# Value products ahead of the next transposes in the attention steps of a two-block transformer kernel

## The reference, cut to what matters

```python
# l0: differential attention, 8 heads, two softmaxes a head
sc = einsum('bqhcd,bkhcd->bhcqk', q_blk, k) * scale
sc = where(causal_mask(i, s), sc + bias, NEG_INF)
a = softmax(sc, axis=-1)
wts = a[:, :, 0] - lam * a[:, :, 1]
return einsum('bhqk,bkhv->bqhv', wts, v)
# l1: latent attention, 16 heads: softmax(where(causal, qn.kn + qp.kp)) @ v
# a:  grouped attention, 16 heads on 4 key heads; 256 tokens see 256 context
#     keys and 256 own keys, and 256 context rows see the 256 context keys
# b:  neighbourhood attention, 16 heads; 256 own keys with a bias, 256 context keys
p = softmax(concatenate([s_nb, s_cx], axis=-1), axis=-1)
return einsum('bqhk,bqkhd->bqhd', p[..., :n_nb], vw) + einsum('bhqs,bshd->bqhd', p[..., n_nb:], vc)
```

## Time and profile before

| | us |
|---|---|
| median of 3 runs | 1422.12 |
| the profiled execution, its own time | 1420.74 |
| its span in the trace | 1418.9 |
| TensorE busy in the span | 1317.7 (93%) |
| VectorE busy | 910.9 (64%) |
| ScalarE busy | 683.4 (48%) |
| granted TensorE clock, mean | 0.981 of full speed |

### The profile page before, as it was taken

The page is one execution under the profiler, slowest core; times in us unless marked ns, Lnnn a source line. Parts: engine busy times, 40 slices in busy tenths (PEclk is TensorE's granted clock), DMA queues, the critical chain, the costliest instruction groups (busy, mean ns, idle before and its releaser), DMA issues.

```text
span 1418.9 us, 24879 instructions
## 1 busy us (share of the span) xinstructions
PE 1317.7 (93%) x9164; PEld 1150.6 (81%) x9164; DVE 910.9 (64%) x1398; ACT 683.4 (48%) x1191; POOL 369.1 (26%) x388
## 2 busy tenths in 40 slices
PE   6989999999998999898999999999989898999777
PEld 4867799999988886798999999788745578889446
DVE  6858667777766887557777778354277437533864
ACT  5554445555544776435555545234376324124651
POOL 5921134333332050232433342111011210000011
PEclk9999999999999999999999999999999998999999
DMA  8565546655643542264656664132200353334100
GB/s 291 177 223 173 181 134 210 183 185 178 182 128 104 164 138 86 102 213 135 218 179 180 186 192 169 60 104 90 89 16 1 83 154 91 103 104 134 30 1 30
DMA packets 52367, 191.58 MB, mean 135 GB/s; under 512 B 6016, under 2 KB 6272, under 8 KB 51904
## 3 DMA queue, kind: packets, MB, share of 16 engines
q1 hardware_dynamic: 43344, 158.85, 36.0%
q0 software_dynamic: 8368, 31.33, 7.1%
q10 hardware_dynamic: 576, 0.31, 0.1%
HBM read 189.41 MB, written 1.05 MB: 134 GB/s over the span
## 4 chain that ended last, share of the span: by engine, by line
PE 76%; DVE 10%; issue 7%; ACT 5%; POOL 1%; DMA 1%; SPq 0%; ACTq 0%; DVEq 0%; POOLq 0%
PE G L394 14%; PE G L396 13%; PE G L395 13%; PE A L394 5%; PE A L396 5%; PE A L395 5%; PE R L514 4%; PE R L559 3%; DVE WL L951 2%; ACT WH L1529 2%; DVE SM L1017 1%; PE A L859 1%; PE R L394 1%; PE G L923 1%; PE R L396 1%
## 5 line engine op out<-in xcount | busy, mean ns | idle before, releaser
L951 DVE TENSOR_TENSOR WL<-RAW,WH 128x1024 fp32r<-128x1024 f32 x295 | 388.2, 1322 | 339.5 <-ACT WH L1529 339.2
L1529 ACT ACTIVATE WH<-RAW 128x1024 fp32r<-128x1024 f32 x295 | 310.4, 1057 | 474.0 <-PE G L396 351.2
L394 PE MATMUL G<-XH,WH 128*128 128x256 f32 (+1 forms) x1408 | 423.7, 301 | 22.6 <-DVE XL L1310 7.5
L395 PE MATMUL G<-XL,WH 128*128 128x256 f32 (+1 forms) x1408 | 420.3, 298 | 0.0
L396 PE MATMUL G<-XH,WL 128*128 128x256 f32 (+1 forms) x1408 | 420.3, 298 | 0.0
L394 PEld LDWEIGHTS G<-XH,WH 128*128 128x128 f32 x1408 | 271.0, 192 | 34.7 <-issue 14.6
L395 PEld LDWEIGHTS G<-XL,WH 128*128 128x128 f32 x1408 | 270.9, 192 | 7.6
L396 PEld LDWEIGHTS G<-XH,WL 128*128 128x128 f32 x1408 | 270.9, 192 | 7.6
L394 PE MATMUL A<-HH,WH 128*128 128x256 f32 x352 | 99.8, 283 | 0.0
L395 PE MATMUL A<-HL,WH 128*128 128x256 f32 x352 | 99.6, 283 | 0.0
L396 PE MATMUL A<-HH,WL 128*128 128x256 f32 x352 | 99.6, 283 | 0.0
(11 more groups left out here) (321 smaller groups left out, 2266.6 us busy)
## 6 DMA issues: line engine op xcount, KB each, us to landing
RAW<-in_wst SPq DMA_DIRECT2D x295, 512.0 KB, 3.7
M<-in_wmod POOLq DMA_DIRECT2D x48, 512.0 KB, 4.6
B<-in_rpb POOLq DMA_DIRECT2D x4, 1024.0 KB, 10.8
H<-in_x_t SPq DMA_DIRECT2D x2, 512.0 KB, 9.2
M<-in_x_tok SPq DMA_DIRECT2D x1, 1024.0 KB, 12.8
M<-in_ctx_t POOLq DMA_DIRECT2D x1, 1024.0 KB, 5.2
out_y<-M SPq DMA_DIRECT2D x1, 1024.0 KB, 3.9
C<-in_cst SPq DMA_DIRECT2D x1, 737.0 KB, 14.7
```

The source lines that it names most:

```text
L394: mm(out, lh, rh, start=start, stop=False, skip_group_check=True)
L395: mm(out, lh, rl, start=False, stop=False, skip_group_check=True)
L951: v.tensor_tensor(WL[:, slot, :], RAW[:, raw, :], WH[:, slot, :].bitcast(F32), ALU.subtract).then_inc(w_lo, 1)
L1529: act(WH[:, slot, :], RAW[:, raw, :], ACT.Copy).then_inc(w_hi, 1)
```

## The change

In `attention` on TensorE the block that issues the value products of unit n-3 is put between the filler and the transposes of unit n-2. Their waits go with them. No other engine's list changes; nothing is added or left out.

```diff
@@ -548,6 +548,13 @@
                         scores(A[2 * (a % 2):2 * (a % 2) + 2], units[n]).then_inc(at_s, 1)
                     if n < len(units) + 2:
                         fill(filler)
+                    if n >= 3 and units[n - 3][4]:
+                        p, qt, nk, job, last = units[n - 3]
+                        pe.wait_ge(at_tc, AU0[s] + n - 2)
+                        j = AJ0[s] + job
+                        if j >= 2:
+                            pe.wait_ge(at_g, j - 1)
+                        value(G[j % 2], att(s, j), units[n - 3]).then_inc(at_pv, 1)
                     if 2 <= n <= len(units) + 1:
                         nk = units[n - 2][2]
                         a = AU0[s] + n - 2
@@ -559,13 +566,6 @@
                                 m = nc.tensor.transpose(ST[c][:, k * P:(k + 1) * P],
                                                         PRB[a % 3][:, c, k * P:(k + 1) * P], IDT)
                         m.then_inc(at_t, 1)
-                    if n >= 3 and units[n - 3][4]:
-                        p, qt, nk, job, last = units[n - 3]
-                        pe.wait_ge(at_tc, AU0[s] + n - 2)
-                        j = AJ0[s] + job
-                        if j >= 2:
-                            pe.wait_ge(at_g, j - 1)
-                        value(G[j % 2], att(s, j), units[n - 3]).then_inc(at_pv, 1)
```

## The result

| | kernel before | changed kernel |
|---|---|---|
| median, first comparison | 1422.12 us (5 runs) | 1428.08 us (5 runs, 1424.98 to 1429.40) |
| ratio, 95% interval | | 1.0051 (1.0034 to 1.0067) |
| median, second comparison | 1421.77 us (21 runs) | 1426.30 us (10 runs, 1422.36 to 1429.16) |
| ratio, 95% interval | | 1.0032 (1.0017 to 1.0047) |
| span of the profiled execution | 1418.9 us | 1426.3 us |

The forecast was 1426.3 us, a loss of 4.2. The medians differ by 6.0 us in the first comparison and by 4.5 in the second. Both intervals lie above 1, so the changed kernel is slower, if only by 0.3 to 0.5%. That the second median is the forecast to the digit is luck: the two medians of the changed kernel lie 1.8 us apart.

What follows compares the result with a forecast made beforehand. Each stage was taken as bound by its closed chain of releases, with TensorE busy for most of the span. Stage a +7.14, its end +0.7, stage b -3.6, l0 and l1 0: +4.2 on 1422.12 gives 1426.3 us, range 1422 to 1431.

Steps and rivals of the forecast that it cites:

- Which chain closes in stage a: Stage a: ten steps through copies, exponentials, transposes and the 16 records make the 10.45 us period; the 8 records are outside.
- The 8 records: Stage a: put ahead, they delay the next u0's transposes by 1.02 us a period, to 11.47; 7 x 1.02 = 7.14.
- The 16 records cost nothing: Stage a: u2's value products and u3's short transposes wait for the same copy, so swapping them costs 0.
- The slack for the delayed exponentials of u1: Stage a: exponentials come 1.45 us later but end 0.7 before VectorE asks; without that slack, up to 10 us in 7 periods.
- The end of a: End of stage a: TensorE waits for the last short copy between the two last value groups, +0.7 us.
- Stage b: Value products fill TensorE's wait; period 7.08 to 6.50 us, then closed over ScalarE; five times plus 0.7 at the end, -3.6.
- b gives nothing: Rival, stage b: later copy and exponentials on ScalarE keep the loop as long as before; 1429.9 us, chance 0.14.
- l0 and l1: Stages l0 and l1: 0 each, as l1's chain holds nothing that moves and l0's TensorE is nearly always busy.
- The copies in a are not what holds it: Rival, stage a: the 8 records cost nothing and b's gain stands; 1418.5 us, chance 0.09.
- waits filled everywhere: Rival, stages a and b: value products fill TensorE's idle time and no other chain closes; -11.4, 1410.7 us, chance 0.03.
- The sum: Whole kernel: 7.14 + 0.7 - 3.6 = +4.2 us, from 1422.12 to 1426.3; own range 1422 to 1431, chance 0.66.
- that sign: Stated sign of being wrong: the granted clock in a stage leaves 0.96 to 0.98 and makes its products longer.

Runs made afterwards that it cites:

- experiment 3: Kernel before, with only the 8 records of the context jobs' value products ahead of the transposes in stage a: ratio 1.0064, 1430.36 us.
- Experiment 4: Kernel before, with only the 16 records of the own-token jobs' value products ahead of the transposes in stage a: ratio 0.9994, 1420.27 us.
- experiment 8: Kernel before, with only the very last swap of stage a (16 records ahead of the last short transposes): ratio 0.9992, 1420.89 us for 1421.77.
- experiment 2: Kernel before, with the new order in stage b alone: ratio 0.9979, 1417.55 us.
- experiment 5: Kernel before, with the new order in stages l0 and l1 alone: ratio 1.0008, 1422.96 us for 1421.03.
- 6: Kernel before, with half of each context job's 8 records ahead of the transposes in stage a: ratio 1.0042, 1427.78 us for 1421.03.
- experiments 1: Kernel before, with the new order in stage a alone: ratio 1.0051, 1428.59 us for 1420.89.
- experiment 9: Kernel before, with stage b's value products split in halves around the transposes and l1 in the new order: ratio 0.9960, 1417.21 us for 1421.03.

## Why the prediction was right

*Which chain closes in stage a.* Right, and shown by experiments, but one argument for it was empty. The prediction adds nine steps between ten starts, finds the period, and takes that as proof that nothing else is in the chain. Differences of starts from one instruction to the same one a period later add up to the period whatever stands between: a list through the 8 records would have done so too. What carries the reading is each link: the earlier trace rows show the copies and the short transposes starting on the release of the member before them, and the other members with no idle time before them. The 8 records are behind the transposes and release nothing that the rows show being waited for. Put ahead of them, they cost their own time: 0.96 a period in the changed kernel and 1.02 in experiment 3.

*The 16 records cost nothing.* Right, and for the reason given: they and the transposes wait for the same copy. Experiment 4 has the period 0.06 shorter. The slack for the delayed exponentials of u1 held: in the changed kernel they start 1.42 later against the transposes of u2 (1.45 forecast), at 1066.06, and end at 1067.07, 0.7 before VectorE's reciprocal at 1067.77, as forecast.

*The end of a.* Right in kind, +0.7 forecast, +0.56 measured in experiment 8.

*Stage b.* Right: period 6.48 for 6.50, closed over ScalarE as worked out with two steps borrowed from stage a, and in experiment 2 -3.5 us at equal clock for -3.6. In the traces, all at clock 1.00, first to last scores take 46.40 us in the changed kernel for 50.05 before, and from the last scores to the first matrix product 13.54 for 13.02 in the old order (experiment 5; 6 and 8 are within 0.01 of it): -3.1 together. With the first part of experiment 2, 48.06 for 52.00 in experiment 5, both at a clock of 0.93, it is -3.4. The profile of the kernel before has 14.66 in place of 13.02, at a clock of 0.88 there, so 1.6 of the 4.9 between the two profiles were the clock's. The rival "b gives nothing" is refuted by experiment 2; it needed 7.08.

*l0 and l1.* Forecast 0 each; together -0.2 us at equal clock in experiment 5. This is a cancelling of two small errors: l0 lost 0.3 and l1 gained 0.6. The prediction had excluded a gain in l1 while its chain stood.

*The copies in a are not what holds it* and *waits filled everywhere* are refuted by experiments 1 and 4. The Trainium skill, "Perfetto Trace Analysis", section "Optimization Strategies", says that the general goal is to keep the matmul engine as highly used as possible. That does not decide the choice here: in stage a both orders give TensorE the same work (512 and 513 records), and what counts is whose turn the engine serves first.

*The sum.* +4.2 forecast, +3.9 at equal clock, +4.5 and +6.0 by the medians. Term by term the traces have 7 x 0.96 = 6.7 for 7.14, 0.56 for 0.7, -3.1 to -3.4 for -3.6, and +0.3 and -0.6 for two zeros: +3.6 to +3.9. No term is off by more than 0.6, and in part the errors cancel. The term that I did not have is the clock. I took equal clocks for granted and named their change only as what would prove me wrong, and that sign did come: 0.92 in stage a and 1.00 in b, outside the stated 0.96 to 0.98. In the first comparison it made up about 3 of the loss: (66.7 - 57.9) x 0.33 = 2.9 us.

*What I missed* is a better order, which the same reading would have given: in b the choice is not only before or behind. Half ahead and half behind leaves both chains shorter than either whole order does, 6.32 us a period.

## What to carry to other kernels

Before moving work ahead on an engine, follow one period back from an instruction to itself, at each step to what released it or, where the engine had no idle time before it, to the instruction ahead of it on its engine. The steps sum to the period for any list, so the sum proves nothing; each link must be free of slack. What is moved ahead of a member of that chain costs its own length unless the engine idled there for something that the moved work does not need too. The same edit can gain in one stage and lose in another, so make it a condition per stage and measure it per stage. Where moving a group ahead and leaving it behind close two different chains, split it between them, and check what the engine's own work in a period comes to: in b it was about 6.2 of the 6.3 us left.

## What the runs showed of the hardware

Runs of one kernel differed by up to 13 us here (1408.69 to 1421.43 in experiment 9), and nearly all of it went with the time that TensorE spent at the lower of its two clock levels (1.2 for 2.4 GHz), 42 to 74 us of a run: 0.33 us for each. The 16 records of value products took 1.95 us at the full level and 3.68 at the lower one, so a stretch bound by TensorE alone would lose near half a microsecond for each; the kernel as a whole lost less. A comparison of kernels that differ by 2 or 3 us in 1420 is clearer at equal clock (scatter 0.8 us) than by medians of runs that scatter by 1.6 to 4.2 us, as long as the change itself is not what moves the clock.
